# The attention pipeline of a streaming encoder step with three score buffers instead of four

## The chip, the cores and the metric

The kernel runs on one core of one Trainium2 chip. The metric is the device time of one execution in microseconds (us): before the change 3189.41 us, the median of three runs (3181.0 to 3197.25). The kernel is written engine by engine: TensorE (PE, with its weight loads PEld), VectorE (DVE), ScalarE (ACT), GpSimd (POOL) and SyncE (SP) each run their own list of instructions strictly in its order, and hand work over by semaphores.

## The reference

A two-layer encoder trunk reads 512 frames of a prompt and 64 frames of a running stream (576 rows of 1024). Layer 0 mixes tokens with a gated MLP, layer 1 with sliding-window attention; behind each stands PEER, in which every row picks 8 x 16 of 16,384 single-neuron experts and adds their outputs. The change touches the attention alone:

```python
s = einsum('bnqkgd,bnskd->bnkgqs', qg, k) * HEAD_DIM ** -0.5
s = s - slopes * dist                       # ALiBi; a chunk of 64 rows sees itself and the two before
p = softmax(concat([s, sink_col], -1), -1)[..., :-1]
o = einsum('bnkgqs,bnskd->bnqkgd', p, v)    # 16 heads of 64, 4 key/value heads
```

The sink column adds one more term, exp(sink - max), to the denominator of each row.

## The kernel before, in words

The 576 rows are five row chunks: 0 to 3 of 128 rows, 4 of 64 rows (the running stream). They are computed as two groups. Group g holds chunks 2, 3, 4 (320 rows) and goes first; its PEER experts are gathered row by row by POOL's indirect DMAs. Group d holds chunks 0 and 1 (256 rows); its experts are computed densely on PE against all experts, streamed from HBM, in a loop of 64 passes in which the gathered steps of group g are worked off too. Layer 1 runs: queries g, attention g, output projection g ("og", L505 to L507), expert selection g, start of the gathers, queries d, attention d, output projection d ("od", L518), selection d, experts.

Attention is cut into units (a list UNITS): one unit is a pair of heads and one row chunk, so attention g has 24 units (8 pairs x 3 chunks, every third with 64 rows) and attention d has 16. A unit n goes through these steps:

1. *scores* (PE, L836): q times k for two heads, into PSUM banks n%2 and 6 + n%2.
2. *max* (DVE, L1745, L1750, L1754): adds the distance term and writes the scores to the buffer S, slot n % SS; row maximum; its negative nm. The writing first waits until the transposes of unit n - SS, which used the slot, are done.
3. *exp* (ACT, L1218, L1220): exponentials in place, with their sum, and the sink's term es.
4. *norm* (DVE, L1762, L1764): denominator and its reciprocal rin. In g, POOL then multiplies both heads' S by rin (L1365); in d, DVE does so itself (L1768).
5. *turn* (PE, L849): transposes S to bank 2 + n%2, behind a wait for step 4 (pn_done).
6. *copy* (ACT, L1231 or L1237): that bank to pT, two buffers.
7. *out* (PE, L871): pT and v to bank 4 + n%2.
8. *evac* (ACT, L1245 in g, L1247 in d), and in g *low* (DVE, L1774), the remainder of a split into two parts.

The order of these steps is written out as a software pipeline: in round n each engine does what belongs to several units. SS, the number of slots of S and of the small per-row values, is 4, and LAG is SS - 1 = 3. In round n PE does scores n, turn n-3, out n-4; ACT does exp n, copy n-3, evac n-4; DVE does max n, norm n-1, low n-5. In d, DVE and ACT also do one gathered expert step (L1628 and L1636; L1094 and L1096) in every odd round, and ACT reloads its function table before and after each.

Of the kernel before, what the change touches and what calls it, by code (L numbers as in the profile page):

```python
# [6 lines left out]
F32, F32R, F16, U32 = mybir.dt.float32, mybir.dt.float32r, mybir.dt.float16, mybir.dt.uint32  # L7
# [4 lines left out]
P = 128  # L12
# [6 lines left out]
HEADS, KVH, DH = 16, 4, 64  # L19
# [134 lines left out]
def program(nc, xT, ckT, cv, gains, lin, uvd, uvg0, uvg1, skT, wsT, bs, sinks, dist, ident_c, iota_a, scaled_c, rank_c,  # L154
# [5 lines left out]
    with ExitStack() as ctx:  # L160
# [9 lines left out]
        def at_(name, off, shape, dt):  # L170
            return nc.alloc_sbuf_tensor_at(name, shape, dt, offset=base + off)
# [11 lines left out]
        g = at_("g", 198656, [P, 2, T], F32)  # L183
# [32 lines left out]
        def arena(*shape, dt=F32):  # L216
# [16 lines left out]

        qT = {"g": at_("qT_g", 18432, [P, DT, TG_], F32), "d": at_("qT_d", 145408, [P, DT, TD], F32)}
        S_ = {"g": at_("S_g", 28672, [P, SS, 2, 2 * P], F32), "d": at_("S_d", 153600, [P, SS, 2, 2 * P], F32)}
        pT_ = {"g": at_("pT_g", 36864, [P, 2, 4, P], F32), "d": at_("pT_d", 87040, [P, 2, 4, P], F32)}
        ck = at_("ck", 40960, [P, 2, P], F32)
        cvs = at_("cvs", 41984, [P, KVH * DH], F32)
        kvs = at_("kvs", 54272, [P, 4, T], F32)
        vnat = at_("vnat", 63488, [P, NTC, KVH * DH], F32)  # L240
        dst = at_("dst", 68608, [P, 2 * P], F32)
        snk = at_("snk", 69632, [P, HEADS], F32)
        mx, nm, den, es, rin = (at_(n, 69696 + 32 * i, [P, SS, 2, 1], F32)
                                for i, n in enumerate(("mx", "nm", "den", "es", "rin")))
# [104 lines left out]
        UNITS = {grp: [(j, c) for j in range(DT) for c in CHUNKS[grp]] for grp in "gd"}  # L349
        UNIT0 = {"g": 0, "d": len(UNITS["g"])}  # L350

        def span(grp, c):

            o = TCO[c] - COLS[grp].start
            return slice(o, o + TCS[c])
# [9 lines left out]
        def keys(c):  # L365

            return (P, [P]) if c == 0 else (0, [P, P]) if c < 4 else (0, [P, DEC])
# [125 lines left out]
        def _(pe):  # L493
# [347 lines left out]
            def att_turn(grp, n):  # L841
                j, c = UNITS[grp][n]
                w, S = TCS[c], S_[grp]
                pe.wait_ge(pn_done, 2 * (UNIT0[grp] + n) + 2)
                pe.wait_ge(free[2 + n % 2], BASE[f"att{grp}"][2 + n % 2] + n // 2)
                for e in range(2):
                    o = 0
                    for m, wk in enumerate(keys(c)[1]):
                        mm = pe.transpose(bank[2 + n % 2][0:wk, P * (2 * e + m):P * (2 * e + m) + w],  # L849
                                          S[0:w, n % SS, e, o:o + wk], ident[0:w, 0:w])  # L850
                        o += wk
                mm.then_inc(full[2 + n % 2], 1)

            def att_out(grp, n):
                j, c = UNITS[grp][n]
                w, pT = TCS[c], pT_[grp]
                base = BASE[f"att{grp}"]
                pe.wait_ge(free[2 + n % 2], base[2 + n % 2] + n // 2 + 1)
                pe.wait_ge(free[4 + n % 2], base[4 + n % 2] + n // 2)
                for e in range(2):  # L860
                    kv = 2 * (j // 4) + e
                    cols = slice(DH * kv, DH * kv + DH)
                    if c == 0:
                        blocks = [vnat[:, 0, cols]]
                    elif c < 4:
                        blocks = [vnat[:, c - 1, cols], vnat[:, c, cols]]
                    else:
                        blocks = [cvs[:, cols], vnat[0:DEC, 4, cols]]
                    for m, vv in enumerate(blocks):
                        wk = keys(c)[1][m]  # L870
                        mm = pe.matmul(bank[4 + n % 2][64 * e:64 * e + 64, 0:w], vv, pT[0:wk, n % 2, 2 * e + m, 0:w],  # L871
                                       start=(m == 0), stop=(m == len(blocks) - 1), skip_group_check=True)
                mm.then_inc(full[4 + n % 2], 1)


            def attention(grp):

                last = BASE[f"q{grp}"]
                for b in range(4):
                    pe.wait_ge(free[b], last[b] + 2)  # L880
                for n in range(len(UNITS[grp]) + LAG + 1):
                    if n < len(UNITS[grp]):
                        att_scores(grp, n)
                    if 0 <= n - LAG < len(UNITS[grp]):
                        att_turn(grp, n - LAG)
                    if 0 <= n - LAG - 1:
                        att_out(grp, n - LAG - 1)
                for b in (4, 5):
                    pe.wait_ge(free[b], BASE[f"att{grp}"][b] + len(UNITS[grp]) // 2)

# [18 lines left out]
        def _(act):  # L909
# [302 lines left out]
            def att_exp(grp, n):  # L1212
                j, c = UNITS[grp][n]
                w, wk, S, u = TCS[c], sum(keys(c)[1]), S_[grp], UNIT0[grp] + n
                for e in range(2):
                    hd = 4 * (2 * (j // 4) + e) + j % 4
                    act.wait_ge(nm_done, 2 * u + e + 1)
                    act.activation(S[0:w, n % SS, e, 0:wk], S[0:w, n % SS, e, 0:wk], ACT.Exp,  # L1218
                                   bias=nm[0:w, n % SS, e, :], accum_out=den[0:w, n % SS, e, :]).then_inc(p_done, 1)
                    act.activation(es[0:w, n % SS, e, :], snk[0:w, hd:hd + 1], ACT.Exp,  # L1220
                                   bias=nm[0:w, n % SS, e, :]).then_inc(es_done, 1)

            def att_copy(grp, n):
                j, c = UNITS[grp][n]
                w, wks, pT = TCS[c], keys(c)[1], pT_[grp]
                base = BASE[f"att{grp}"]
                act.wait_ge(full[2 + n % 2], base[2 + n % 2] + n // 2 + 1)
                if n >= 2:
                    act.wait_ge(full[4 + n % 2], base[4 + n % 2] + n // 2)
                if wks == [P, P]:  # L1230
                    act.activation(pT[:, n % 2, :, :], bank[2 + n % 2][:, :].rearrange("p (a q) -> p a q", a=4),  # L1231
                                   ACT.Copy).then_inc(free[2 + n % 2], 1)
                    return
                src = bank[2 + n % 2][:, :].rearrange("p (e m q) -> p e m q", e=2, m=2)
                dstp = pT[:, n % 2, :, :].rearrange("p (e m) q -> p e m q", e=2)
                for m, wk in enumerate(wks):
                    a = act.activation(dstp[0:wk, :, m, 0:w], src[0:wk, :, m, 0:w], ACT.Copy)  # L1237
                a.then_inc(free[2 + n % 2], 1)

            def att_evac(grp, n):  # L1240
                j, c = UNITS[grp][n]
                b = 4 + n % 2
                act.wait_ge(full[b], BASE[f"att{grp}"][b] + n // 2 + 1)
                if grp == "g":
                    act.activation(xh[:, j, span(grp, c)], bank[b][:, 0:TCS[c]], ACT.Copy).then_inc(oh_done, 1)  # L1245
                else:
                    act.activation(xd[:, j, span(grp, c)], bank[b][:, 0:TCS[c]], ACT.Copy).then_inc(free[b], 1)  # L1247

            def attention(grp):

                for n in range(len(UNITS[grp]) + LAG + 1):
                    if n < len(UNITS[grp]):
                        att_exp(grp, n)
                    if 0 <= n - LAG < len(UNITS[grp]):
                        att_copy(grp, n - LAG)
                    if 0 <= n - LAG - 1:
                        att_evac(grp, n - LAG - 1)
                    if grp == "d":
                        weights_at(1, f"att{n}")

# [114 lines left out]
        def _(dve):  # L1375
# [395 lines left out]
            def att_low(n):  # L1771
                j, c = UNITS["g"][n]
                dve.wait_ge(oh_done, n + 1)
                dve.tensor_tensor(xl[:, j, span("g", c)], bank[4 + n % 2][:, 0:TCS[c]],  # L1774
                                  xh[:, j, span("g", c)].bitcast(F32), ALU.subtract).then_inc(free[4 + n % 2], 1)

            def attention(grp):

                for n in range(len(UNITS[grp]) + LAG + 2):
                    if n < len(UNITS[grp]):  # L1780
                        att_max(grp, n)
                    if 0 <= n - 1 < len(UNITS[grp]):
                        att_norm(grp, n - 1)
                    if 0 <= n - LAG - 2 and grp == "g":
                        att_low(n - LAG - 2)
                    if grp == "d":
                        steps_at(1, f"att{n}")

# [17 lines left out]


HEAD = 2
SS = 4
LAG = SS - 1  # L1810


# [67 lines left out]
```

## Time and profile before

| what | value |
|---|---|
| time, median of three runs | 3189.41 us (3181.0 to 3197.25) |
| time of the profiled execution | 3189.41 us |
| its span in the trace | 3187.6 us |
| PE busy | 2941.6 us (92%) |
| DVE busy | 2469.6 us (77%) |
| ACT busy | 813.6 us (26%) |
| POOL busy | 1034.3 us (32%) |
| attention g, first scores to first projection matmul | 1635.02 to 1705.37 us |
| attention d, first scores to first projection matmul | 1856.59 to 1923.38 us |

The profile is one execution. Busy shares are means over stages with different limits; the two attention stages together are about 137 us of the span. A number in a row of the trace is the start in us from the span's start, then the time taken.

### The profile page before, as it was taken

Reading aid. Unit: us, or ns where it says so; the run is one execution under the profiler, and the core shown is the slowest. Engines: PE = TensorE matmul, PEld = TensorE weight load, DVE = VectorE, ACT = ScalarE, POOL = GpSimd, SP = SyncE. Lnnn points to the kernel's source line nnn. Section 1 sums busy time; section 2 is a strip of 40 time slices with the busy share of each in tenths; the row PEclk is TensorE's granted clock in tenths of the full one; section 3 lists DMA queues with packets and bytes.
Section 4 is the critical chain, followed back from the end, with each engine's and each line's share of the span. In section 5 each row is a group of like instructions: output and inputs, shape, how many; then the busy total and the mean of one; then the engine's idle time right before and its main releaser. Section 6 shows DMA issues by size and latency. Waiting matters only on the chain.

```text
span 3187.6 us, 46747 instructions
## 1 busy us (share of the span) xinstructions
PE 2941.6 (92%) x17342; PEld 2573.7 (81%) x17342; DVE 2469.6 (77%) x5415; ACT 813.6 (26%) x2398; POOL 1034.3 (32%) x840
## 2 busy tenths in 40 slices
PE   8898999999999999987878978979999999999977
PEld 7797888888888888865666957868888888888865
DVE  2466798988888888887654776998888888888878
ACT  5332222211211111111355362222211112111112
POOL 6432122333332333333365321122322333333332
PEclk9799998999999999998988968989999999999989
DMA  5226777899999999999622257668999999999997
GB/s 188 78 98 251 261 296 299 355 421 422 421 422 420 416 421 418 411 412 421 234 82 66 92 192 271 261 255 308 415 421 422 421 421 415 421 418 410 414 421 298
DMA packets 159968, 1042.99 MB, mean 327 GB/s; under 512 B 18481, under 2 KB 23921, under 8 KB 44097
## 3 DMA queue, kind: packets, MB, share of 16 engines
q0 software_dynamic: 92160, 671.13, 51.6%
q1 hardware_dynamic: 63648, 357.59, 28.8%
q10 hardware_dynamic: 4000, 12.36, 1.1%
q8 instruction: 74, 1.21, 0.1%
q14 instruction: 86, 0.70, 0.1%
HBM read 1033.28 MB, written 7.86 MB: 327 GB/s over the span
## 4 chain that ended last, share of the span: by engine, by line
DMA 40%; PE 38%; DVE 13%; issue 7%; ACT 2%; POOL 0%; DVEq 0%; SPq 0%; ACTq 0%; POOLq 0%
DMA gata<-uvg,idxg 27%; DMA gatb<-uvg,idxg 12%; PE bank L715 10%; PE bank L518 8%; DVE acc L1636 6%; PE bank L728 3%; PE bank L505 3%; PE bank L702 3%; PE bank L507 3%; PE bank L506 3%; PE bank L604 1%; DVE gata L1628 1%; PE bank L535 1%; DMA U<-uvd 1%; PE bank L583 1%
## 5 line engine op out<-in xcount | busy, mean ns | idle before, releaser
L728 PE MATMUL bank<-a,V 128*128 128x256 f32 x4096 | 935.3, 388 | 75.4 <-DVE a L1619 70.3
L728 PEld LDWEIGHTS bank<-a,V 128*128 128x128 f32 x4096 | 796.4, 195 | 197.7 <-issue 73.9
L715 PE MATMUL bank<-xd,U 128*128 128x256 f32 x4096 | 936.7, 388 | 4.4 <-DMA U<-uvd 4.4
L1299 POOL DMA_INDIRECT gata<-uvg,idxg x428 | 515.5, 1205 | 1251.5 <-DVE acc L1636 1191.9
L715 PEld LDWEIGHTS bank<-xd,U 128*128 128x128 f32 x4096 | 787.5, 195 | 112.2 <-DMA U<-uvd 5.7
L1628 DVE CUSTOM_DVE_ANT_0 gata<-gata,xrow 128x1024 f32<-128x1024 f32 x428 | 522.7, 1221 | 218.9 <-DMA gata<-uvg,idxg 213.9
L1636 DVE SCALAR_TENSOR_TENSOR acc<-gata,wgt,acc 128x1024 f32<-128x1024 f32 x428 | 548.2, 1281 | 27.2 <-ACT wgt L1096 27.0
L1094 ACT ACTIVATE act<-dot 128x1 f32<-128x1 f32 x640 | 129.5, 202 | 1581.6 <-DVE dot L1628 1581.6
L1299 POOL DMA_INDIRECT gatb<-uvg,idxg x212 | 244.4, 1153 | 567.1 <-DVE acc L1636 558.0
L1628 DVE CUSTOM_DVE_ANT_0 gatb<-gatb,xrow 128x1024 f32<-128x1024 f32 x212 | 258.9, 1221 | 105.2 <-DMA gatb<-uvg,idxg 104.0
L702 PEld LDWEIGHTS bank<-B,oneA 128*128 128x128 f16 x4096 | 279.2, 150 | 35.1 <-DVE oneA L1602 14.0
L702 PE MATMUL bank<-B,oneA 128*128 128x32 f16 x4096 | 283.1, 246 | 19.7 <-DVE oneA L1602 13.7
L1636 DVE SCALAR_TENSOR_TENSOR acc<-gatb,wgt,acc 128x1024 f32<-128x1024 f32 x212 | 271.6, 1281 | 1.1 <-ACT wgt L1096 1.1
L518 PE MATMUL bank<-xd,raw 128*128 128x256 f32 x1088 | 251.1, 388 | 7.5 <-DVE xd L1398 7.1
L518 PEld LDWEIGHTS bank<-xd,raw 128*128 128x128 f32 x1088 | 209.3, 195 | 37.6 <-issue 9.0
L505 PE MATMUL bank<-xh,wh 128*128 128x320 f32 x608 | 201.1, 331 | 28.5 <-POOL xl L412 24.6
L1096 ACT ACTIVATE wgt<-act,gateg 128x1 f32<-128x1 f32 x640 | 189.3, 296 | 20.9
L506 PE MATMUL bank<-xl,wh 128*128 128x320 f32 x608 | 191.6, 315 | 0.0
L507 PE MATMUL bank<-xh,wl 128*128 128x320 f32 x608 | 191.4, 315 | 0.0
L1602 DVE TENSOR_TENSOR oneA<-iotaA,i 128x1024 f16<-128x1024 f16 x256 | 168.5, 698 | 0.0
L1333 POOL TENSOR_TENSOR wl<-raw,wh 128x1024 fp32r<-128x1024 f32 x48 | 116.1, 2420 | 103.3 <-ACT wh L925 103.2
L505 PEld LDWEIGHTS bank<-xh,wh 128*128 128x128 f32 x608 | 117.6, 193 | 39.4 <-issue 32.8
(198 smaller groups left out, 2506.6 us busy)
## 6 DMA issues: line engine op xcount, KB each, us to landing
U<-uvd SPq DMA_DIRECT2D x128, 1024.0 KB
V<-uvd SPq DMA_DIRECT2D x128, 1024.0 KB
raw<-lin SPq DMA_DIRECT2D x152, 512.0 KB
gata<-uvg,idxg POOLq DMA_INDIRECT x428
hsp<-h ACTq DMA_DIRECT2D x2, 2304.0 KB, 12.9
hx<-hsp SPq DMA_DIRECT2D x2, 2304.0 KB, 16.5
gatb<-uvg,idxg POOLq DMA_INDIRECT x212
sk_g<-skT ACTq DMA_DIRECT2D x2, 1024.0 KB, 4.8
```

The source lines that it names most:

```text
L505: pe.matmul(out, whi, xh[:, k, :], start=(k == 0), stop=False)
L506: pe.matmul(out, whi, xl[:, k, :], start=False, stop=False)
L507: mm = pe.matmul(out, wlo, xh[:, k, :], start=False, stop=(k == DT - 1))
L518: mm = pe.matmul(bank[s][:, 0:TD], raw[:, s, P * k:P * k + P], x[:, k, :], start=(k == 0), stop=(k == DT - 1))
L702: mm = pe.matmul(bank[2 + s][:, CHUNK * t:CHUNK * (t + 1)], oneA[:, s, t // TG, :, t % TG], B[:, s, part, :, t], start=(t == 0 and part == ...
L715: mm = pe.matmul(bank[s][:, TD * t:TD * t + TD], U[:, s, o:o + P], xd[:, k, :], start=(t == 0 and k == 0), stop=(k == DT - 1), skip_group_ ...
L728: mm = pe.matmul(bank[b][:, TD * (d % 2):TD * (d % 2) + TD], V[:, s, o:o + P], a[:, s, TD * k:TD * k + TD], start=(first and k == 0 and d ...
L1096: act.activation(wgt[:, k:k + 1], act8[:, k:k + 1], ACT.Copy, scale=gateg[:, s:s + 1])\
L1299: pool.indirect_dma_start(row(l, s), None, uvg[l], bass.IndirectOffsetOnAxis(idxg[:, s:s + 1], 0)).then_inc(g_in[s % SLOTS], 16)
L1602: ins = dve.tensor_tensor(oneA[:, s, u], iotaA[:, :, :], i1[:, None, t + TG * u:t + TG * u + TG].broadcast_to([P, P, TG]), ALU.is_equal)
L1628: dve.tensor_tensor_reduce(u, u, xrow[:, min(s // P, 2), :], 1.0, 0.0, ALU.mult, ALU.add, dot[:, s % 8:s % 8 + 1]).then_inc(dot_done, 1)
L1636: dve.scalar_tensor_tensor(out=acc[:, n, :], in0=row(l, s)[:, D:RD], scalar=wgt[:, s % 8:s % 8 + 1], in1=acc[:, n, :], op0=ALU.mult, op1=A ...
```

## The change

SS goes from 4 to 3, and the name LAG is replaced by the number 2 in the three attention loops. Per round PE now does scores n, turn n-2, out n-3; ACT exp n, copy n-2, evac n-3; DVE max n, norm n-1, low n-4. Each loop has one round less. S of group g shrinks from 8 KB to 6 KB per partition, and three buffers behind it (pT_g, ck, cvs) move down by 2 KB; nothing is put in the space.

```diff
-        pT_ = {"g": at_("pT_g", 36864, [P, 2, 4, P], F32), "d": at_("pT_d", 87040, [P, 2, 4, P], F32)}
-        ck = at_("ck", 40960, [P, 2, P], F32)
-        cvs = at_("cvs", 41984, [P, KVH * DH], F32)
+        pT_ = {"g": at_("pT_g", 34816, [P, 2, 4, P], F32), "d": at_("pT_d", 87040, [P, 2, 4, P], F32)}
+        ck = at_("ck", 38912, [P, 2, P], F32)
+        cvs = at_("cvs", 39936, [P, KVH * DH], F32)
...
-                for n in range(len(UNITS[grp]) + LAG + 1):
+                for n in range(len(UNITS[grp]) + 3):
                     if n < len(UNITS[grp]):
                         att_scores(grp, n)
-                    if 0 <= n - LAG < len(UNITS[grp]):
-                        att_turn(grp, n - LAG)
-                    if 0 <= n - LAG - 1:
-                        att_out(grp, n - LAG - 1)
+                    if 0 <= n - 2 < len(UNITS[grp]):
+                        att_turn(grp, n - 2)
+                    if 0 <= n - 3:
+                        att_out(grp, n - 3)
...
-                    if 0 <= n - LAG < len(UNITS[grp]):
-                        att_copy(grp, n - LAG)
-                    if 0 <= n - LAG - 1:
-                        att_evac(grp, n - LAG - 1)
+                    if 0 <= n - 2 < len(UNITS[grp]):
+                        att_copy(grp, n - 2)
+                    if 0 <= n - 3:
+                        att_evac(grp, n - 3)
...
-                    if 0 <= n - LAG - 2 and grp == "g":
-                        att_low(n - LAG - 2)
+                    if 0 <= n - 4 and grp == "g":
+                        att_low(n - 4)
...
-SS = 4
-LAG = SS - 1
+SS = 3
```

How the order moves, first on PE near the start of attention g. S_g is the score buffer, qT_g the queries, kvs and ck the keys, vnat the values, pT_g the turned probabilities. Before, from the scores of unit 3 to those of unit 5:

```order
L836 MATMUL bank<-kvs,qT_g 128x256 [waits free1]
L836 MATMUL bank<-kvs,qT_g 128x256 [waits free7]
L849 MATMUL bank<-ident,S_g 128x128 [waits free2,pn_done]
L849 MATMUL bank<-ident,S_g 128x128 x3
L836 MATMUL bank<-kvs,qT_g 128x256 [waits free0]
L836 MATMUL bank<-kvs,qT_g 128x256 [waits free6]
L849 MATMUL bank<-ident,S_g 128x128 [waits free3,pn_done]
L849 MATMUL bank<-ident,S_g 128x128 x3
L871 MATMUL bank<-pT_g,vnat 64x128 [waits free4,free2]
L871 MATMUL bank<-pT_g,vnat 64x128 x3
L836 MATMUL bank<-ck,qT_g 64x128 [waits free1]
```

And the changed kernel on PE from the same place:

```order
L849 MATMUL bank<-ident,S_g 128x128 [waits free2,pn_done]
L849 MATMUL bank<-ident,S_g 128x128 x3
L836 MATMUL bank<-kvs,qT_g 128x256 [waits free1]
L836 MATMUL bank<-kvs,qT_g 128x256 [waits free7]
L849 MATMUL bank<-ident,S_g 128x128 [waits free3,pn_done]
L849 MATMUL bank<-ident,S_g 128x128 x3
L871 MATMUL bank<-pT_g,vnat 64x128 [waits free4,free2]
L871 MATMUL bank<-pT_g,vnat 64x128 x3
L836 MATMUL bank<-kvs,qT_g 128x256 [waits free0]
L836 MATMUL bank<-kvs,qT_g 128x256 [waits free6]
L849 MATMUL bank<-ident,S_g 128x64 [waits free2,pn_done]
```

The scores of unit 3 (free1 and free7) now stand behind the transposes of unit 0 and their wait for pn_done; each later unit's scores likewise stand behind the transposes of a unit one later than before.

On ACT at the same place, before (exp of units 2 and 3, then the first copy; nm is the negative maximum, es the sink's term):

```order
L1218 ACTIVATE S_g,den<-S_g,nm 64x192 [waits nm_done]
L1220 ACTIVATE es<-snk,nm 64x1
L1218 ACTIVATE S_g,den<-S_g,nm 128x256 [waits nm_done]
L1220 ACTIVATE es<-snk,nm 128x1
L1218 ACTIVATE S_g,den<-S_g,nm 128x256 [waits nm_done]
L1220 ACTIVATE es<-snk,nm 128x1
L1231 ACTIVATE pT_g<-bank 128x512 [waits full2]
```

And in the changed kernel:

```order
L1218 ACTIVATE S_g,den<-S_g,nm 64x192 [waits nm_done]
L1220 ACTIVATE es<-snk,nm 64x1
L1231 ACTIVATE pT_g<-bank 128x512 [waits full2]
L1218 ACTIVATE S_g,den<-S_g,nm 128x256 [waits nm_done]
L1220 ACTIVATE es<-snk,nm 128x1
L1218 ACTIVATE S_g,den<-S_g,nm 128x256 [waits nm_done]
L1220 ACTIVATE es<-snk,nm 128x1
```

The first copy now stands ahead of the exponentials of unit 3; no instruction is added or dropped on any engine.

## Rows read from the trace of the kernel before

**Rows 1.** The page, part 4: shares of the chain that ended last.

```profile
DMA 40%; PE 38%; DVE 13%; issue 7%; ACT 2%; POOL 0%; DVEq 0%; SPq 0%; ACTq 0%; POOLq 0%
```

**Rows 2.** Windows: length, each engine's busy us and count, granted clock, DMA share, GB/s.

```profile
1634.00:1706.00 72.00, 54.11 (x422) 36.05 (x423) 50.69 (x194) 49.70 (x201) 43.31 (x49) 0.86 0.06 20
1855.00:1924.00 69.00, 43.12 (x240) 25.75 (x238) 53.35 (x168) 54.30 (x160) 15.35 (x14) 0.57 0.55 206
```

**Rows 3.** Waits in attention g: who waited for whom, us, times, longest.

```profile
PE bank L871 <- ACT pT_g L1231: 10.3, 12, 1.3
```

**Rows 4.** Timeline, steady part of attention g: start, us, engine, instruction, [idle before].

```profile
1674.01 0.70 PE L836 MATMUL bank<-kvs,qT_g 64*128 64x256 f32 x4
1674.64 0.66 PE L849 MATMUL bank<-ident,S_g 128*128 128x128 f32 x4
...
1674.81 0.75 DVE L1745 SCALAR_TENSOR_TENSOR S_g<-dst,bank 128x256 f32<-128x256 f32 x2 [0.41 <-PE bank L836]
...
1676.39 0.34 DVE L1754 TENSOR_SCALAR nm<-mx,snk 128x1 f32<-128x1 f32 x2
...
1676.63 0.51 ACT L1218 ACTIVATE S_g<-S_g,nm 128x256 f32<-128x256 f32 x1 [0.93 <-DVE nm L1754]
...
1676.82 0.16 DVE L1764 RECIPROCAL rin<-den 64x2 f32<-64x2 f32 x1
...
1677.07 1.50 POOL L1365 TENSOR_SCALAR S_g<-S_g,rin 64x192 f32<-64x192 f32 x2 [0.94 <-DVE rin L1764]
...
1678.00 0.58 ACT L1231 ACTIVATE pT_g<-bank 128x512 f32<-128x512 f32 x1
...
1678.63 0.67 PE L871 MATMUL bank<-pT_g,vnat 128*64 128x128 f32 x8 [0.72 <-ACT pT_g L1231]
...
1679.23 0.44 PE L836 MATMUL bank<-ck,qT_g 64*64 64x128 f32 x4
...
1679.70 1.83 POOL L1365 TENSOR_SCALAR S_g<-S_g,rin 128x256 f32<-128x256 f32 x2 [1.13 <-DVE rin L1764]
...
1679.71 0.45 PE L849 MATMUL bank<-ident,S_g 64*128 64x64 f32 x4
```

**Rows 5.** Timeline, first rounds of attention g.

```profile
1642.89 1.12 PE L849 MATMUL bank<-ident,S_g 128*128 128x128 f32 x4 [3.57 <-POOL S_g L1365]
...
1643.93 1.23 PE L836 MATMUL bank<-kvs,qT_g 64*128 64x256 f32 x4
...
1645.26 0.75 DVE L1745 SCALAR_TENSOR_TENSOR S_g<-dst,bank 128x256 f32<-128x256 f32 x2 [0.52 <-PE bank L836]
...
1646.40 1.13 PE L871 MATMUL bank<-pT_g,vnat 128*64 128x128 f32 x8 [0.20 <-ACT pT_g L1231]
...
1647.46 0.70 PE L836 MATMUL bank<-ck,qT_g 64*64 64x128 f32 x4
```

**Rows 6.** Timeline, last scores of attention g and first matmul of og.

```profile
1695.20 0.44 PE L836 MATMUL bank<-ck,qT_g 64*64 64x128 f32 x4
...
1705.37 0.38 PE L505 MATMUL bank<-xh,wh 128*128 128x320 f32 x1 [0.62 <-issue]
```

**Rows 7.** Windows of 4 us, columns as in rows 2.

```profile
1648.00:1652.00 4.00, 3.90 (x26) 2.56 (x22) 2.44 (x10) 3.03 (x14) 2.91 (x4) 0.50 0.00 0
...
1684.00:1688.00 4.00, 3.00 (x24) 2.03 (x26) 3.04 (x14) 3.25 (x14) 2.25 (x3) 0.82 0.00 0
...
1900.00:1904.00 4.00, 3.93 (x22) 2.72 (x24) 3.89 (x12) 3.73 (x13) 0.13 (x1) 0.50 0.67 252
```

**Rows 8.** Timeline of attention d: one steady round and the end.

```profile
1887.26 0.36 ACT L1237 ACTIVATE pT_d<-bank 128x256 f32<-128x256 f32 x1
...
1891.42 0.74 DVE L1745 SCALAR_TENSOR_TENSOR S_d<-dst,bank 128x256 f32<-128x256 f32 x2
...
1918.21 0.62 DVE L1768 TENSOR_SCALAR S_d<-S_d,rin 128x256 f32<-128x256 f32 x2
...
1923.38 2.80 PE L518 MATMUL bank<-xd,raw 128*128 128x256 f32 x7 [0.43 <-issue]
```

More of the change, by code:

```diff
@@ L1249, in attention @@
             def attention(grp):
-                for n in range(len(UNITS[grp]) + LAG + 1):
+                for n in range(len(UNITS[grp]) + 3):
                     if n < len(UNITS[grp]):
                         att_exp(grp, n)
-                    if 0 <= n - LAG < len(UNITS[grp]):
-                        att_copy(grp, n - LAG)
-                    if 0 <= n - LAG - 1:
-                        att_evac(grp, n - LAG - 1)
+                    if 0 <= n - 2 < len(UNITS[grp]):
+                        att_copy(grp, n - 2)
+                    if 0 <= n - 3:
+                        att_evac(grp, n - 3)
                     if grp == "d":
@@ L1777, in attention @@
             def attention(grp):
-                for n in range(len(UNITS[grp]) + LAG + 2):
+                for n in range(len(UNITS[grp]) + 4):
                     if n < len(UNITS[grp]):
```

## The prediction

> **What bounds the kernel now.** I first read the page's chain: 40% of it is DMA and 38% PE [rows 1]. Both belong mostly to the expert stages, which the change doesn't touch. What it touches are two stages of about 70 us each, so I read their windows next [rows 2]: in attention g no engine is busy all the time (PE 54.1 of 72 us, DVE 50.7, ACT 49.7), which means that a cycle over several engines sets the pace; in attention d ACT (54.3 of 69) and DVE (53.4) are the fullest. Both stages lie on the one path of layer 1: group g's selection needs attention g, the dense expert loop needs attention d. A microsecond won or lost there should therefore go to the end one to one.
>
> The waits of attention g name one link of the cycle: PE waits 10.3 us in 12 pieces for ACT's copy of the turned probabilities [rows 3]. The timeline gives the rest [rows 4]. Follow it from the scores of one unit, call it k: scores k start 1674.01; DVE takes them up at 1674.81 (+0.80); the negative maximum comes at 1676.39 (+1.58); ACT starts exp k at 1676.63 (+0.24); only behind it, at 1678.00 (+1.37), ACT copies unit k-3; PE starts out k-3 at 1678.63 (+0.63) and scores k+2 at 1679.23 (+0.60). Sum 5.22 us for two units, 2.61 a unit. This is the old cycle. Nothing in it depends on how far apart exp and copy are in units: it says that the copy stands behind the exp of the same round, and out one round behind the copy. With two rounds' distance instead of three it stays as it is, 2.61 a unit.
>
> **The change, part by part.** No instruction is added or removed. Three things move.
>
> *1. The turn in attention g.* In round k PE does scores k, and then turns unit k-2 instead of k-3. Unit k-2 gets its reciprocal on DVE in round k-1, behind the maximum of unit k-1, and then goes through POOL. Before, POOL had a round more. Take the rows as they stand: the POOL instruction pair that starts at 1677.07 ends at 1678.57, the one before it ended by about 1676.1 (start a quarter of a microsecond behind its reciprocal, 1.83 long). PE came to the turn of that round at 1674.64 [rows 4]. Had it been the turn of unit k-2, PE would have stood for about 1.5 us, and behind it, in PE's list, stand out k-3 and scores k+1, for which DVE waits. So a second cycle closes: scores k-1 to DVE 0.80, to the negative maximum 1.58, to the reciprocal 0.43 (1676.39 to 1676.82), to POOL 0.25 (to 1677.07), POOL 1.83 (the row at 1679.70), the semaphore 0.05, the turn 0.61 (0.66 less the overlap at its end), out 0.60, and then scores k+1: 6.15 us for two units, against 5.22. A third of the units have 64 rows: there POOL takes 1.50 instead of 1.83 (0.11 less on the mean) and the turn 0.45 instead of 0.66 (0.07 less), and the old cycle is about 0.09 shorter for its copy. The difference is 0.93 - 0.18 + 0.09 = 0.84 us for two units, 0.42 a unit. The old wait for the copy is then hidden: copy k-2 ends about 7.6 us behind scores k-1, and PE, which turns the next unit first, asks for it at about 8.6.
>
> How many units? Before, the first turn starts at 1642.89, held by POOL, and the scores behind it at 1643.93 are those of unit 4 [rows 5]. After, the same turn stands in front of unit 3, whose scores then start at 1643.93. The last scores (unit 23) started at 1695.20 [rows 6]: 19 units in 51.27 us, 2.70 each, low clock at the start included. After, it is 20 units. Each takes 2.70 + 0.42, and about 0.04 more for the share of the stage at the low clock, in which the turn that is now on the cycle takes 1.04 instead of 0.61 (1642.89 to 1643.93). That makes 3.16 x 20 = 63.2 us.
>
> *2. The end of attention g.* From the last scores to the first matmul of og it took 10.17 us [rows 6], four rounds with three turns. After, there is one round less. From the last scores, by the rows: DVE needs 2.4 us to the reciprocal of unit 22, POOL until 4.5 for it and, queued behind, until 6.0 for unit 23; turn, out (64 rows, about 1.1) and the two small copies end near 8.6, og at 8.9; with part of it at the low clock I take 9.2. So the stage from 1643.93 to og is 63.2 + 9.2 = 72.4 us, where it was 61.44: +11.0 us.
>
> *3. Attention d.* DVE multiplies by the reciprocal itself, so the turn of unit k-2 never waits longer than DVE's own list. What may go wrong is that scores come late. In an odd round ACT starts its copy at 1887.26 [rows 8]; it is now that of a two-block unit and takes 0.58 instead of 0.36. Out follows (1.06, from 1646.40 to 1647.46 at the low clock [rows 5]) and then the next scores (1.23), which end at about 1890.1. DVE asks for them at 1891.42 [rows 8]: 1.3 us to spare, where it was 2.4. So DVE's list goes on setting the pace and nothing is lost per round. At the end one round goes: the last product ends at 1918.83 (1918.21 + 0.62), turn (1.1), copy (0.6), out (1.1) and 0.7 for the last copy and the step to od make 1922.3 instead of 1923.38: -1.1 us. Bounds for d: -1.3 if the low clock is lifted there, and +9 if the 1.3 us are missed by as much again in each of 7 pairs of rounds. I take -1.1, since the walk leaves the margin.
>
> The moved buffers cost nothing: same shapes and partitions. Sum: 11.0 - 1.1 = +9.9 us on 3189.41, the time of the profiled execution, which is also the median of the three runs: **3199 us**. The three runs lie up to 8 us off their median, so that is close to what repeats can tell.
>
> **The clock.** The granted clock of attention g was 0.50 from 1648 to 1652 with PE busy 3.90 of 4 us, and dipped again between 1684 and 1688 (0.82) though PE was busy for 3.00 of 4 [rows 7]. In attention d it was 0.50 even in a window with 3.93 of 4 us busy [rows 7], and 0.57 on the mean [rows 2]. 0.50 is 1.2 GHz, 1.00 is 2.4. So the level is not certain, and the new wait makes PE idle about 0.4 us more per unit. The price of the low level is worked out from rows 5: scores to DVE 1.33 instead of 0.80, turn 1.04 instead of 0.61, out 1.06 instead of 0.60, so the new cycle is 6.15 + 1.42 = 7.57 for two full units, about 3.57 a unit with the 64-row ones in it.
>
> The Trainium skill (TensorE: Matmul & The Clock Gate, "Part 1: The HAM clock gate") says that the throttled level is the default and that sustained activity of the PE lifts it. By it, a stage in which PE idles more would be the likelier to stay at 1.2 GHz. The rows bear this out only in part, as they show the low level beside a nearly full PE too. It is the first rival.
>
> **The rivals.**
>
> *A. The clock stays at 1.2 GHz through attention g.* For it: PE has more gaps, and attention d, with a longer gap in each pair of rounds, ran at 0.57. Against it: the first rounds of g recovered, and at the low level PE would be busy for 3.33 (1.23 + 1.04 + 1.06) of the 3.79 us of a full unit. Time: 20 x 3.57 + 11 = 82.4 us instead of 61.4, +21.0, with d -1.1: +19.9, **3209 us**, slower by 0.6%.
>
> *B. The wait only takes the place of another.* PE waited 10.3 us for the copy [rows 3]; if the wait for POOL overlaps it and the rows' distances shrink under it, 2.61 a unit stays, and only the shorter ends are left: about -1.3 in g and -1.1 in d, **3187 us**. Against it: 6.15 is more than 5.22, and each link of it is a row. This is the side of "not slower"; the point from which it decides is a new cycle of at most 5.22, that is a path from the reciprocal to the end of the turn of 1.8 us and not of 2.74.
>
> *C. Attention d loses its margin* (the bound above): the new order puts the copy that PE needs behind ACT's exp, and if scores come 1.3 us late in each of 7 pairs, DVE idles and the stage takes 9 us more: 11.0 + 9 = +20, **3209 us**. Against it: the walk has them 1.3 us early.
>
> **How the numbers follow.** Forecast 0.62, A 0.17, B 0.13, C 0.08. For the likeliest the time is 3199 (own range 3193 to 3205, somewhat less than the 8 us by which single runs lay off their median). The range runs from B to beyond A: 3187 to 3212. A measurement of this kernel can tell about 0.5%, 16 us, from no change. +9.9 lies inside; A and C lie at +20, just outside, and scatter adds some of the forecast's case. So slower by over 0.5%: 0.25; within: 0.71; faster: 0.04.
>
> **What would show it.** In the new profile, attention g: PE waits for POOL at L849 in nearly every round, about 1 us and more each, and its waits at L871 for L1231 all but vanish; scores of one unit follow those of the one before by 3.0 to 3.2 us; POOL and DVE are less busy per us. From first scores to og 81 us instead of 70.35. Attention d: the same pairs of rounds, od one microsecond earlier after the first scores. The experts as before. Wrong would be: no wait at L849 (then B), a clock at 0.5 through g (A), DVE waiting for L836 in d (C), or a change of the time in the expert stages.

## The result, and the profile after

The changed kernel takes 3209.22 us, median of 12 runs (3204.33 to 3217.05), against 3190.76 us of the kernel before (12 runs, 3181.0 to 3202.56). The ratio is 1.0061, 95% interval 1.005 to 1.0074: slower by 0.6%, some 18 to 20 us. The profiled execution has a span of 3212.2 us, 24.6 us more than the one of before.

Where the 24.6 us lie can be read from starts on PE. The first scores of attention g start 0.5 us earlier than before. From them to the first matmul of og (1634.52 to 1728.39) it takes 93.87 us instead of 70.35: +23.5. From og to the first scores of attention d, 151.3 us instead of 151.2. Attention d (1879.67 to 1945.19) takes 65.52 instead of 66.79: -1.3. From there to the end, 1267.0 instead of 1264.2: +2.8. So nearly the whole change lies in attention g. The 2.8 us are within scatter: in the fourteen profiles of this document the stretch behind attention d, whose instructions are the same in all, took 1264.2 to 1271.3 us, and the kernel before had the shortest.

The windows of both attention stages in the profile after, columns as in [rows 2]:

```profile
1634.00:1728.00 94.00, 73.34 (x416) 47.72 (x416) 50.47 (x192) 50.75 (x201) 42.78 (x49) 0.56 0.05 15
1880.00:1945.00 65.00, 42.28 (x208) 23.74 (x204) 53.00 (x168) 53.76 (x159) 15.43 (x14) 0.53 0.58 209
```

DVE, ACT and POOL do the same work as before [rows 2] over a longer time. PE is busy 73 us instead of 54 for the same matmuls, and the third figure from the end goes with it: the granted clock fell from 0.86 to 0.56. The waits of attention g after (who waited for whom, us in total, times, longest), which answer to [rows 3]:

```profile
POOL S_g L1365 <- DVE rin L1764: 47.7, 22, 4.9
DVE S_g L1745 <- PE bank L836: 32.9, 20, 3.7
...
PE bank L849 <- POOL S_g L1365: 19.8, 16, 5.7
```

The same wait at the turn was a single one before, that of the first turn:

```profile
PE bank L849 <- POOL S_g L1365: 3.6, 1, 3.6
```

The wait of out for ACT's copy, 10.3 us before, no longer appears. In its place PE waits 19.8 us at the turn (L849) for POOL, and POOL itself waits 47.7 us for reciprocals: no engine is busy all the time, and a cycle over PE, DVE and POOL sets the pace. The chain that ended last shows it. Three units of attention g in the profile after (start, us, what):

```profile
1669.23 1.16 PE bank L836 x3
...
1670.48 0.76 DVE S_g L1745 x2
...
1671.34 0.70 DVE mx L1750
...
1672.19 0.20 DVE nm L1754
...
1672.50 0.18 DVE rin L1764
...
1672.76 1.84 POOL S_g L1365 x2
...
1674.64 1.11 PE bank L849 x4
1675.75 1.62 PE bank L871 x8
1677.37 1.15 PE bank L836 x4
1678.52 1.04 PE bank L849 x4
1679.56 1.06 PE bank L871 x8
1680.62 1.16 PE bank L836 x3
```

The window of these rounds:

```profile
1668.00:1682.00 14.00, 12.11 (x65) 7.44 (x64) 7.75 (x31) 7.60 (x32) 6.22 (x8) 0.50 0.00 1
```

The path runs from scores over DVE and POOL to the turn, as predicted. But it doesn't close after two units: from that turn PE is never idle for the rest of two rounds (out, scores, turn, out, scores), and the cycle closes after three units and 1680.62 - 1669.23 = 11.39 us, 3.80 a unit. At this level of the clock (0.50, which is 1.2 GHz) more of PE's own work stands on the cycle than the prediction had there. The out of the unit with 64 rows takes 1.62 us there, where the one with 128 rows takes 1.06.

The scores of unit 3 (the fourth), the last scores and the first matmul of og in the profile after, which answer to [rows 5] and [rows 6]:

```profile
1643.43 1.23 PE L836 MATMUL bank<-kvs,qT_g 64*128 64x256 f32 x4
...
1718.10 0.70 PE L836 MATMUL bank<-ck,qT_g 64*64 64x128 f32 x4
...
1728.39 0.38 PE L505 MATMUL bank<-xh,wh 128*128 128x320 f32 x1 [0.62 <-issue]
```

### The profile page after: what moved, and what is told of

It is laid out like the page before. It is cut to its first block, busy times and chain, and to the rows that moved or that the text cites. A ratio compares the mean times of both kernels' runs of the same rounds, so it can differ in the third digit from the quotient of the medians.

```text
span 3212.2 us, 46749 instructions
## 1 busy us (share of the span) xinstructions
PE 2966.7 (92%) x17342; PEld 2589.3 (81%) x17342; DVE 2472.0 (77%) x5415; ACT 814.0 (25%) x2398; POOL 1018.7 (32%) x840
## 4 chain that ended last, share of the span: by engine, by line
DMA 41%; PE 37%; DVE 13%; issue 7%; ACT 1%; POOL 1%; DVEq 0%; ACTq 0%; POOLq 0%
DMA gata<-uvg,idxg 23%; DMA gatb<-uvg,idxg 17%; PE bank L715 9%; PE bank L518 8%; DVE acc L1636 6%; PE bank L505 3%; PE bank L507 3%; PE bank L506 3%; PE bank L702 3%; PE bank L728 2%; PE bank L604 1%; PE bank L535 1%; DVE gata L1628 1%; DMA U<-uvd 1%; PE bank L871 1%
## 5 line engine op out<-in xcount | busy, mean ns | idle before, releaser
L1299 POOL DMA_INDIRECT gata<-uvg,idxg x428 | 507.6, 1186 | 1266.6 <-DVE acc L1636 1205.6
L1299 POOL DMA_INDIRECT gatb<-uvg,idxg x212 | 236.7, 1116 | 570.3 <-DVE acc L1636 562.6
```

Of the source, the lines that this page charges most:

```text
L1299: pool.indirect_dma_start(row(l, s), None, uvg[l], bass.IndirectOffsetOnAxis(idxg[:, s:s + 1], 0)).then_inc(g_in[s % SLOTS], 16)
```

## The experiments

A ratio is to runs of the kernel before made beside it, with its 95% interval; 0.1% is 3.2 us. "Attention g" is the time from its first scores to the first matmul of og in the run's one profile. Windows have the columns of [rows 2]; the granted clock is the third figure from the end.

**Which of the two stages.** `g_only` and `d_only` keep four slots and put the distance of two rounds in one group only:

```diff
-LAG = SS - 1
+LAGS = {"g": 2, "d": 3}    # g_only;  d_only: {"g": 3, "d": 2};  LAG becomes LAGS[grp] in the loops
```

> Distance of two rounds in attention g alone, four slots of S in both groups, attention d as before. If attention g carries the cost, the time is that of the changed kernel plus the one microsecond that d's shorter end gave: +19 to +20 on before (3210), attention g from first scores to og some 93 us. If d carries a part (rival C), clearly less than +18.

> Distance of two rounds in attention d alone, four slots, attention g as before. Theory: in d the distance only shortens the end, so the stage takes 65.5 instead of 66.8 us and the kernel is 1 us faster, which these rounds can't tell from none: within 0.2% of before. Rival C (the margin of 1.3 us for the scores is lost): up to +9 us, and waits of DVE for the scores (L836) in d.

Measured: `g_only` 1.0052 (1.0034 to 1.0071), attention g 92.4 us; `d_only` 0.9997 (0.9982 to 1.0011), attention d 65.75 us. Their windows of attention g:

```profile
1626.00:1719.00 93.00, 70.10 (x417) 45.76 (x418) 50.31 (x193) 50.73 (x201) 42.49 (x49) 0.61 0.05 15
```

```profile
1626.00:1704.00 78.00, 64.00 (x418) 42.14 (x419) 49.98 (x192) 49.69 (x201) 42.30 (x49) 0.69 0.06 17
```

Attention g carries the cost, and d gives its microsecond back, which only the stage's length shows (66.9 us in `g_only`). The second row says more: `d_only` has attention g exactly as before, and there the stage took 77.6 us at a clock of 0.69, where the profile before had 70.35 at 0.86. So the old order doesn't hold the high clock either; the profile on which the prediction rests caught it in a good execution. The granted clock over the whole span, which is known for every run beside the experiments, says the same: 76 runs of the kernel before had 0.939 to 0.955, half of them under 0.947, and the lower it was the longer they took (a median of 3203 us for the 16 runs up to 0.942, of 3184 us for the 5 from 0.951). The profile before had 0.948, `d_only` 0.945, the 37 runs of the changed kernel 0.937 to 0.944.

**Slots or distance.** `four_slots` is the changed distance with the old buffers:

```diff
-LAG = SS - 1
+LAG = 2                    # SS stays 4
```

> Four slots of S kept, distance of two rounds in both groups. Theory (the turn waits for POOL one round too early): same as the changed kernel, 3209, since no instruction waits for a slot. Rival (the third slot is missing: DVE waits for the transposes before it may write S): the time comes back to about 3191.

Measured: 1.0051 (1.0034 to 1.0067), attention g 90.8 us, PE's wait for POOL at L849 21.8 us:

```profile
1627.00:1717.00 90.00, 67.87 (x416) 43.95 (x412) 50.04 (x191) 50.49 (x201) 41.78 (x49) 0.64 0.04 13
```

The buffer count plays no part; the order does. The buffers also stand at their old addresses here, so moving them cost nothing that can be told from none.

**POOL's place in the cycle.** `no_pool`:

```diff
-                pe.wait_ge(pn_done, 2 * (UNIT0[grp] + n) + 2)
+                pe.wait_ge(p_done if grp == "g" else pn_done, 2 * (UNIT0[grp] + n) + 2)
...
                 for e in range(2):
-                    pool.tensor_scalar(S[...], S[...], rin[...], None, ALU.mult).then_inc(pn_done, 1)
+                    pool.nop().then_inc(pn_done, 1)
```

This kernel leaves out the division by the softmax's denominator in group g. The turn now waits for the exponentials (p_done), so both POOL and DVE's reciprocal are off the path to it.

> The changed kernel, POOL's multiplication in attention g left out (the probabilities stay undivided there) and the turn waiting for the exponentials only. Theory: the cycle over POOL is gone, so PE's wait at the turn goes, the old cycle of 2.6 us a unit comes back with ends shorter by 1 to 2 us: 3186 to 3191, attention g 68 to 70 us. Rival (the shorter pipeline or the low clock alone is the cause, POOL is not): stays near 3209.

Measured: 0.9997 (0.9983 to 1.0011), so the whole cost is gone, as the theory has it. The length of the stage was a miss, 78 us where 68 to 70 were expected:

```profile
1627.00:1705.00 78.00, 65.08 (x416) 43.75 (x416) 49.65 (x192) 49.58 (x201) 1.19 (x1) 0.67 0.06 16
```

That is the length and the clock of the old order in `d_only`. Without reciprocal and POOL in the cycle the pipeline of distance two is as fast as the old one, low clock included. The edit doesn't part the two.

**The clock by itself.** `fill_after` and `fill_before` add two matmuls per unit whose result is overwritten ("idle matmuls"), in front of the wait where PE idles. In `fill_after`:

```diff
+                pe.wait_ge(free[2 + n % 2], BASE[f"att{grp}"][2 + n % 2] + n // 2)
+                if grp == "g":
+                    for _ in range(2):
+                        pe.matmul(bank[2 + n % 2][:, 0:256], ident[:, :], kvs[:, 0, 0:256], start=True, stop=True,
+                                  skip_group_check=True)
                 pe.wait_ge(pn_done, 2 * (UNIT0[grp] + n) + 2)
-                pe.wait_ge(free[2 + n % 2], BASE[f"att{grp}"][2 + n % 2] + n // 2)
```

In `fill_before` the same two stand in front of out's wait for the copy and write its bank, 4 + n%2.

> The changed kernel with two idle matmuls (128x256, results overwritten) in front of each turn's wait for POOL in attention g, so that PE has work there. Nothing else. Theory with the clock as the multiplier: granted clock of the stage rises from 0.56 to above 0.85, a unit takes 3.0 to 3.1 us instead of 3.8, the stage about 78 instead of 94 us, the kernel 3194 to 3200, faster than the changed kernel though it does more work. Rival (the clock is a by-product and costs nothing): more work on PE, the kernel at 3209 or up to 15 us above it (48 matmuls of about 0.3 to 0.6 us).

> The kernel before with the same two idle matmuls per unit, here in front of out's wait for the copy in attention g (where it idled 0.7 to 1.1 us). Theory: granted clock of the stage from 0.85 to above 0.95, attention g 66 to 70 us instead of 70.4, the kernel 0 to 4 us faster than before. So the clock was not worth much in the kernel before, and is worth some 15 us only together with the shorter distance. Rival (filling gains in any pipeline): 10 us or more faster.

Measured: `fill_after` 1.0004 (0.9991 to 1.0016), attention g 80.9 us; `fill_before` 1.0014 (1.0 to 1.0029), attention g 74.6 us. First `fill_after`, then `fill_before`:

```profile
1635.00:1716.00 81.00, 71.19 (x513) 48.34 (x513) 50.31 (x192) 49.89 (x201) 42.28 (x49) 0.96 0.06 17
```

```profile
1633.00:1708.00 75.00, 69.38 (x514) 47.94 (x514) 50.17 (x192) 49.82 (x201) 42.35 (x49) 0.95 0.06 18
```

48 useless matmuls take the changed kernel from 1.0061 back to the time of before. That is the plainest evidence that the lower clock makes up a good part of the cost, as nothing in the order got shorter. Two rows of its trace, the scores of unit 3 and of unit 23, give the rate:

```profile
1644.02 1.23 PE L836 MATMUL bank<-kvs,qT_g 64*128 64x256 f32 x4
...
1706.43 0.44 PE L836 MATMUL bank<-ck,qT_g 64*64 64x128 f32 x4
```

That is 62.41 us for 20 units, 3.12 each, against 3.73 in the changed kernel. `fill_before` was a miss: 66 to 70 us and a small gain were expected, the stage took 74.6 us and the kernel was no faster. A pair of idle matmuls takes PE 1.06 us, and with them PE is busy for 69.4 of 75 us, so there was too little idle time to hide them. What the high clock alone is worth in the old order is therefore not measured here. With the filling in both orders the stage is 6.3 us longer at distance two, but the times of the whole kernels (1.0004 and 1.0014) don't show a difference.

**Filling only the first gap.** `burst_after` puts ten such matmuls once, in front of the first turn (`if grp == "g" and n == 0`), where PE idles 5.7 us in the profile after and the clock falls to 0.50.

> The changed kernel with ten idle matmuls (5.3 us at the high clock) only once, in front of the first turn of attention g, where PE idles some 6 us. Theory a (the clock is lost in this one gap and then not regained): the clock stays high for the stage, which takes some 80 us, the kernel 3195 to 3200, as with idle matmuls in every round. Theory b (the gaps of each round keep the clock low): it falls again within the stage, the clock of the stage is below 0.8, the time stays above 3205.

Measured: 1.0053 (1.0035 to 1.0071), attention g 91.0 us. Windows within it:

```profile
1640.00:1652.00 12.00, 7.70 (x58) 5.39 (x57) 7.44 (x29) 8.41 (x36) 6.95 (x8) 0.91 0.01 5
1652.00:1668.00 16.00, 14.21 (x74) 8.97 (x72) 7.85 (x33) 8.16 (x33) 6.96 (x8) 0.50 0.00 1
1668.00:1696.00 28.00, 19.46 (x139) 12.65 (x139) 17.81 (x70) 16.96 (x71) 13.85 (x17) 0.74 0.00 1
```

Theory b holds: the stage starts at the high clock, falls after 1648 and wavers from then on. Filling the first gap alone doesn't keep the clock in the new order; filling the wait of every round did.

**The old cycle, cut.** `copy_first_before` and `copy_first_after` change ACT's order in a round of g:

```diff
-                    if n < len(UNITS[grp]):
+                    if grp == "d" and n < len(UNITS[grp]):
                         att_exp(grp, n)
                     ...                             # att_copy, att_evac as they were
+                    if grp == "g" and n < len(UNITS[grp]):
+                        att_exp(grp, n)
```

> The kernel before with ACT's order in a round of attention g turned round: copy n-3, evac n-4, then exp n. The old cycle needs the copy behind the exp; this cuts it. Left are the engines' own lists, DVE's 2.3 us a unit. Theory: 2.3 to 2.4 us a unit, attention g 63 to 66 us, the kernel 5 to 8 us faster than before. Rival (the cycle is set by another link, or the clock stays low and PE's own 3.2 us a unit bind): no gain or a loss.

> The changed kernel with the same turned order on ACT in g (copy n-2, evac n-3, exp n). Theory: the copy is not on the cycle over POOL, so nothing comes back: 3209 to 3216, attention g 90 to 94 us; it may get worse, as the exp now stands behind a copy that waits for the late turn. Rival B (the wait for POOL only took the place of the wait for the copy, and both are one): the time falls to that of before.

Measured: with distance three 0.9972 (0.9958 to 0.9986), attention g 68.2 us; with distance two 1.0057 (1.0037 to 1.0078), attention g 93.7 us, PE's wait for POOL 23.1 us. The gain of 0.28% (8.9 us, interval 4.5 to 13.4) is what was expected, the stage of 68.2 us is not (63 to 66). So the cycle through ACT bound before, at least in part, and has no part in the changed kernel. Two windows of `copy_first_before`, the low and the high level:

```profile
1636.00:1656.00 20.00, 20.00 (x109) 12.59 (x108) 12.64 (x51) 13.65 (x55) 12.04 (x15) 0.50 0.00 1
1660.00:1684.00 24.00, 20.80 (x188) 13.73 (x186) 21.69 (x88) 21.79 (x92) 18.59 (x23) 1.00 0.01 2
```

At 1.2 GHz PE is busy all the time and binds; at 2.4 GHz DVE and ACT are both just over 90% busy, and which of them binds wasn't tested.

**Versions that beat both.** `burst_copy_first` adds six idle matmuls before the first turn to that order. `copy_first_deeper` instead gives g a distance of four with five slots. `deeper_burst` has both.

```diff
-SS = 4
-LAG = SS - 1
+SL = {"g": 5, "d": 4}
+LAGS = {"g": 4, "d": 3}
```

The diff is against the kernel before; with it S of group g and the small per-row values get five slots, and the three buffers behind S_g move up by 2 KB.

> Distance three, four slots, copy ahead of exp on ACT in g, and six idle matmuls once in front of the first turn. Without them this order took 68.2 us for attention g, 28 us of it at the low clock with PE full. Theory: the low clock is avoided or shorter, the stage 62 to 65 us, the kernel 3179 to 3182, 8 to 13 us faster than before. Rival: the clock falls anyway, 3184 as without.

> Copy ahead of exp on ACT in g with a distance of four rounds and five slots in g (d unchanged at three and four). Theory: POOL has a round more, the 6.4 us that PE waited at L849 go, the rate was already DVE's 2.3 us a unit in the second half, the end is a round longer: 3182 to 3186, no clear difference from the order with distance three. Rival (distance is worth as much upwards as it cost downwards, 10 us a round): 3175.

> Copy ahead of exp on ACT in g, distance four and five slots in g, and six idle matmuls once in front of the first turn. With distance four alone the stage took 62.4 us, its first 20 us at the low clock with PE full; with the burst at distance three 62.3 us. Theory: the two add up only in part, since DVE's list of 2.3 us a unit stands under both: 24 x 2.3 + 6 = 61 us at the least, so 60 to 62 us and 3176 to 3179 us. Rival (they add up fully): the stage 57 us, the kernel 3172.

| kernel | ratio to before | 95% interval | attention g, us |
|---|---|---|---|
| burst_copy_first | 0.9955 | 0.9939 to 0.9972 | 62.3 |
| copy_first_deeper | 0.9947 | 0.9931 to 0.9964 | 62.4 |
| deeper_burst | 0.9951 | 0.9932 to 0.997 | 59.8 |

`burst_copy_first` came out as expected, with the clock at 0.92. `copy_first_deeper` was a miss: it was expected to be no better than distance three, and its stage is 5.8 us shorter. The intervals of the two kernels (0.9931 to 0.9964 and 0.9958 to 0.9986) still overlap. Its windows:

```profile
1636.00:1652.00 16.00, 15.34 (x91) 10.81 (x92) 12.43 (x48) 12.93 (x54) 12.14 (x15) 0.50 0.01 1
1656.00:1684.00 28.00, 22.78 (x226) 15.90 (x224) 25.59 (x105) 25.98 (x112) 22.43 (x27) 1.00 0.01 2
```

It, too, starts at the low clock; DVE is at 25.6 of 28 us afterwards. How much of the 5.8 us is owed to the deeper order and how much to a clock that came back a little sooner in this execution, one profile can't say. The stage of `deeper_burst` is the shortest, but 2.6 us are below what the runs of the whole kernel resolve: the three intervals overlap. The first two are about 15 us faster than before. For `deeper_burst` the ratio says as much, with an interval from 10 to 22 us, while the medians differ by only 10.8 us (3184.34 and 3195.16).

## Why the prediction was right or wrong

The measured time is inside the range and on rival A's 3209 us, not on the forecast's 3199. The order of events was forecast rightly; the fall of the clock that came with it was not. In order of its steps:

1. *The old cycle through the copy, 5.22 us for two units.* Right for the high clock: cutting it (`copy_first_before`) gained 0.28%, and the same cut did nothing once POOL was in the cycle. At the low clock PE's own list binds instead, as the windows of `copy_first_before` show.
2. *The turn comes a round too early for POOL, and scores are queued behind it.* Right: `no_pool` takes the whole cost away (with reciprocal and POOL together), `four_slots` shows that slots are not it, the waits at L849 are there and those at L871 for the copy are gone.
3. *The size at the high clock, +11 us in attention g.* It fits the only run of this order at that clock: `fill_after` took 80.9 us at 0.96 against 81.4 by the sum (70.35 + 11.0), 3.12 us a unit against 3.16. But its idle matmuls stand in front of some turns that didn't have to wait, so this is not the changed kernel's own rate, and an agreement this close is partly luck.
4. *The rate of 3.16 us a unit, with the clock of the profile before.* This is the step that failed: the forecast's term for the low clock, 0.04 us a unit. In the profile after, 20 units from 1643.43 to 1718.10 took 74.67 us, 3.73 each, at a clock of 0.56 for the stage. The prediction carried over the share of the stage at the low clock from one execution in which it was small; two other executions with the same or an equivalent cycle had 0.69 and 0.67. It gave the low clock 17 in 100, though the trace before showed attention d at 0.57 with gaps in each pair of rounds. Why the clock falls further in the new order is open: filling the waits holds it at 0.96, but it was also low with PE nearly full (last section).
5. *The price of the low level, rival A: 3.57 us a unit, 82.4 us from the fourth scores to og.* Measured 3.80 in the chain, 3.73 on the mean and 84.96 us. The sum took the cycle of two units and out at 1.06 us for the 64-row unit; the binding cycle spans three units, passes PE's list twice and holds an out of 1.62. So rival A's own sum was 2.6 us short in g, and that its 3209 us met the measured 3209.22 is luck: the sum starts from an execution in which the stage took 70.35 us, where `d_only` shows 77.6 for the same order.
6. *The end of g, 9.2 us.* 10.3 us measured, at the low clock. The end of d: -1.1 forecast, -1.3 in the profile, -1.0 in `d_only`.
7. *Attention d keeps its pace.* Right, rival C is out: 65.5 to 65.8 us in every kernel with distance two there, and the waits for scores (L836) come to 0.2 us. Rival B is out by `copy_first_after`.

The runs show +18.5 us and the two profiles +24.6. The profile of the changed kernel was taken in an execution that was 4.8 us above the median of its runs (3213.98 against 3209.22), that of the kernel before in one 1.3 us below its own; that makes the difference of 6.1. Of the 24.6 us, 2.8 are the stretch behind attention d. The clock of a run without a profile is known over the whole span only, so how long attention g was at the low clock in those runs stays open.

## What to carry to other kernels

In a pipeline written out by hand over in-order queues, look for the cycles, with the number of rounds each spans. A shorter distance cost nothing in attention d, where the scores still came in time. In attention g the wait moved in front of scores that DVE needed, which closed a longer cycle and cost time in every unit; the slot that went with it was not what was lost. And where the TensorE clock wavers in a stage, one profile of it is one draw: price the stage at both levels, give the lower one real weight, and look at a second execution.

## What the runs showed of the hardware

The low clock went together with a PE whose records are full. In `copy_first_before` PE was busy 20.00 of 20 us between 1636 and 1656 us at a granted clock of 0.50 (1.2 GHz), and the clock rose only after 1656. `d_only`, with the old order in g, shows nearly the same:

```profile
1668.00:1696.00 28.00, 26.92 (x149) 17.66 (x150) 17.36 (x70) 17.18 (x71) 14.18 (x17) 0.50 0.00 1
```

In attention d the clock was 0.53 to 0.59 in every kernel. The Trainium skill (TensorE: Matmul & The Clock Gate, "Part 1: The HAM clock gate") has it that activity lifts the throttle. These two stretches don't bear that out. In the other direction the trace agrees: idle matmuls in each round brought the stage to 0.96, and made a kernel with more work 0.6% faster.
